# Paged sample attention in a hybrid decoder step: value products placed directly ahead of the scores two blocks on, value loads ahead of key loads

## What is computed

```python
k_past = cache_k[page_table].reshape(Bs, past_len, N_HEADS_B, HEAD_DIM_B)
v_past = cache_v[page_table].reshape(Bs, past_len, N_HEADS_B, HEAD_DIM_B)
...
z = jnp.einsum("bqhd,bkhd->bhqk", q_i.astype(f32), kf) * scale + bias
mask = (k_pos[None, :] < p_i[:, None])[None, None]
log_keep = jnp.where(mask, jax.nn.log_sigmoid(-z), 0.0)
log_rest = lax.cumsum(log_keep, axis=3, reverse=True) - log_keep
att = jnp.where(mask, jnp.exp(jax.nn.log_sigmoid(z) + log_rest), 0.0)
return jnp.einsum("bhqk,bkhd->bqhd", att, vf)
```

## Time and profile before

| what | value |
|---|---|
| median of 3 runs | 2033.95 us |
| lowest, highest | 2031.24, 2036.3 us |
| profiled execution: span from first to last instruction | 2041.4 us |
| mean granted TensorE clock, share of full speed | 0.978 |
| busy share of the span: PE, PEld, DVE, ACT, POOL | 93%, 80%, 50%, 40%, 12% |
| DMA: moved, mean rate | 505.53 MB, 248 GB/s |
| key loads of 1024 KB: issue to landing, median | 11.2 us |
| value loads of 1024 KB: issue to landing, median | 10.7 us |
| weight loads of 1024 KB: issue to landing, median | 6.1 us |

### The profile page before, as it was taken

How to read it: one execution, slowest core, us unless ns; L and a number is a source line. 1 busy time by engine, 2 the same in 40 slices (tenths; PEclk the granted TensorE clock), 3 DMA queues, 4 the chain that set the end, 5 groups by cost and what they waited for, 6 DMA issues and landing times.

```text
span 2041.4 us, 49327 instructions
## 1 busy us (share of the span) xinstructions
PE 1900.4 (93%) x20670; PEld 1626.6 (80%) x20670; DVE 1014.2 (50%) x1676; ACT 816.9 (40%) x1436; POOL 244.5 (12%) x308
## 2 busy tenths in 40 slices
PE   7999999999999999999999999999999899777797
PEld 6988999999888888879998777677777677334597
DVE  6644363544455555534454553343454344677344
ACT  4234232334455555623333333333333344655333
POOL 0200000000244434413200000000000000110032
PEclk9999999999999999989999999999999999998899
DMA  7435455544123222205488999999999999999641
GB/s 282 172 134 178 161 177 172 170 163 151 55 89 101 86 89 76 58 18 192 145 322 303 419 419 420 394 425 425 425 425 425 397 418 386 416 384 359 258 144 73
DMA packets 122382, 505.53 MB, mean 248 GB/s; under 512 B 15969, under 2 KB 55266, under 8 KB 76898
## 3 DMA queue, kind: packets, MB, share of 16 engines
q1 hardware_dynamic: 122178, 502.60, 64.4%
HBM read 470.24 MB, written 32.32 MB: 246 GB/s over the span
## 4 chain that ended last, share of the span: by engine, by line
PE 29%; DMA 18%; DVE 2%; issue 2%; SPq 1%; ACT 1%; DVEq 0%; ACTq 0%
DMA at_vraw<-in_cache_v 18%; PE psP L2499 7%; PE psP L2501 7%; PE psP L2500 7%; PE at_psO L2549 4%; PE at_psS L2528 3%; SPq L1912 1%; PE psP L2594 0%; PE at_psT L2540 0%; SPq L1930 0%; SPq L1952 0%; DVE at_o_new L2416 0%; ACT at_p_w L2219 0%; PE psP L2616 0%; ACT at_p_w L2217 0%
## 5 line engine op out<-in xcount | busy, mean ns | idle before, releaser
L2499 PE MATMUL psP<-xhi,whi 128*128 128x320 f32 x1488 | 476.3, 320 | 2.6 <-DVE xlo L2386 1.9
L2500 PE MATMUL psP<-xlo,whi 128*128 128x320 f32 x1488 | 461.0, 310 | 0.0
L2501 PE MATMUL psP<-xhi,wlo 128*128 128x320 f32 x1488 | 461.0, 310 | 0.0
L2499 PEld LDWEIGHTS psP<-xhi,whi 128*128 128x128 f32 x1488 | 280.8, 189 | 65.8 <-issue 65.1
L2261 DVE TENSOR_TENSOR wlo<-wraw,whi 128x2048 fp32r<-128x2048 f32 x92 | 213.0, 2315 | 206.8 <-ACT whi L2087 206.6
L2087 ACT ACTIVATE whi<-wraw 128x2048 fp32r<-128x2048 f32 x92 | 176.0, 1913 | 277.0 <-PE psP L2501 275.7
L2500 PEld LDWEIGHTS psP<-xlo,whi 128*128 128x128 f32 x1488 | 281.2, 189 | 0.1
L2501 PEld LDWEIGHTS psP<-xhi,wlo 128*128 128x128 f32 x1488 | 280.8, 189 | 0.0
L131 PE MATMUL psP<-xhi,whi 128*128 128x320 f32 x704 | 218.1, 310 | 3.0 <-DVE wlo L166 2.4
L132 PE MATMUL psP<-xlo,whi 128*128 128x320 f32 x704 | 217.5, 309 | 0.0
L133 PE MATMUL psP<-xhi,wlo 128*128 128x320 f32 x704 | 217.5, 309 | 0.0
(11 more groups left out here) (359 smaller groups left out, 3237.0 us busy)
## 6 DMA issues: line engine op xcount, KB each, us to landing
wraw<-in_weights SPq DMA_DIRECT2D x160, 1024.0 KB, 6.1
at_kraw<-in_cache_k SPq DMA_DIRECT2D x96, 1024.0 KB, 11.2
at_vraw<-in_cache_v SPq DMA_DIRECT2D x94, 1024.0 KB, 10.7
at_kraw<-in_cache_k SPq DMA_DIRECT2D x64, 512.0 KB, 9.7
at_vraw<-in_cache_v SPq DMA_DIRECT2D x62, 512.0 KB, 10.7
rw_s0t<-in_s0T SPq DMA_DIRECT2D x16, 256.0 KB, 4.0
o_wkv_s<-rw_SN SPq DMA_DIRECT2D x16, 256.0 KB, 2.2
resT<-in_xT SPq DMA_DIRECT2D x4, 640.0 KB, 5.9
```

The lines of the kernel that those rows point to most:

```text
L2499: pe.matmul(out, wh, c_.xhi[:, kc, :], start=(kc == 0), stop=False)
L2500: pe.matmul(out, wh, c_.xlo[:, kc, :], start=False, stop=False)
L2501: last = pe.matmul(out, wl, c_.xhi[:, kc, :], start=False, stop=(kc == NM - 1))
```

## The change

One function is new, and six places use it. The values of block `k`, and what hangs on them, are planned from `value_time` and not from `block_time(k, 1.5)`:

```diff
+def value_time(k, part=0.0):
+
+    return block_time(k, part + (1.995 if k < NK - 2 else 1.5))
+
+
 def sample_ended(b):
-    return block_time(NBLK * max(b, SHARING - 1) + NBLK - 1, 2.3)
+    return value_time(NBLK * max(b, SHARING - 1) + NBLK - 1, 0.8)
...
-                values = [(block_time(freed // KB, 1.6 + 0.2 * (freed % KB)), load_value, i // KB, i % KB)
+                values = [(value_time(freed // KB, 0.02 + 0.02 * (freed % KB)), load_value, i // KB, i % KB)
                           for i in range(VRING + 1, KB * (NK - 1)) for freed in (i - VRING - (i < EXTRA + 4),)]
...
             def finals():
                 for b in range(NB):
-                    yield block_time(NBLK * b + NBLK - 1, 1.9)
+                    yield value_time(NBLK * b + NBLK - 1, 0.4)
...
-                    yield block_time(NBLK * b + NBLK - 1, 2.25)
+                    yield value_time(NBLK * b + NBLK - 1, 0.75)
...
-                    yield block_time(k, 1.5)
+                    yield value_time(k)
                     pe.wait_ge(*((v_in[k % 2], loads_of(k)) if k < NK - 1 else (v_last, 16 * KB)))
...
                     if k % NBLK == NBLK - 1:
-                        yield block_time(k, 2.2)
+                        yield value_time(k, 0.7)
```

## The result

The change makes the kernel slower: 2063.72 us (median of 4 runs), against 2035.12 us for the kernel before on the same chip (4 runs), a ratio of 1.0125 with a 95% interval of 1.0099 to 1.0152. One of the four runs was a slow one, 4663.27 us; the other three took 2060.38, 2062.49 and 2064.94 us, and the ratio goes by these. The forecast was 2028.5 us with a range of 2020 to 2040 us, so it was wrong in its direction and its range. The profiled execution took 2064.94 us, its span is 2063.2 us, and its mean granted clock is 0.969 (0.978 before).

A forecast was written before the change was run, and what follows sets the result against it. Transfers were taken to bound the kernel from 1120 to 1905 us. Taking back 5.5 us of the DMA engines' dry time, with all other terms at 0, gave 2033.95 - 5.5 = 2028.5 us, range 2020 to 2040 us.

The forecast's parts named there:

- the bound of the stretch beside the heads: Beside the prompt's heads, transfers were taken as the bound, with DMA share 0.98 over 165 us.
- In steady flow this costs and gives nothing: Moving values directly ahead of scores on PE keeps the load order and was costed at 0 in steady flow.
- That stretch is full at 0.98, so this gives nothing by itself: Beside the heads, ending PE's 8.0 us of waits for ACT's copy saves no time, as transfers fill the stretch.
- rival D: PE's clock falls behind longer waits for value pages, slowing values to scores: up to +9 us, 2043 us; chance 0.17.
- rival A: The forecast itself: the DMA engines' dry time from 1120 to 1905 us shrinks, gaining 2 to 9.4 us; chance 0.52.
- No window with a share under 0.8: Sign of the forecast being right: no 5 us window from 1120 to 1905 us has a DMA share under 0.8.
- Fewer changes of matmul kind: On PE, 0.31 us saved for each of 62 blocks, 19 us, all spent waiting for values; costed at nothing.
- rival C: PE was the hidden bound, so the 19 us of matmul switches come off: 2015 us; chance 0.13.
- Turn and values apart: Among the heads, PE's 8.0 us of waits for ACT's copy of turned weights go; value pages are late next; gain 0.
- Value loads ahead of key loads: On SP, weight chunks and stores move ahead of the value loads; no transfer gets longer, cost nothing.
- Start and end: At the kernel's start 0, bounds -2 and +3 us; at its end 0, bound +2 us.
- A's fastest case: Lower end of the time range that the shrinking dry time alone gives, 2023.5 to 2032 us.

The follow-up runs named there:

- run 7: Kernel before, with only an eighth of every key and value page loaded from block 48 on: 2028.6 us (one run); scores 48 to 63 take 172.7 us.
- run 8: Changed kernel, with only an eighth of every key and value page loaded from block 48 on: 2053.86 us (one run); scores 48 to 63 take 206.5 us.
- run 1: Change kept for blocks 0 to 46 only, blocks 47 to 61 as in the kernel before: 2031.44 us, ratio 0.9963 to the kernel before.
- run 2: Change kept for blocks 47 to 61 only, blocks 0 to 46 as in the kernel before: 2067.42 us, ratio 1.0148 to the kernel before.
- run 3: Changed kernel's place of the values on PE, with all loads in the order of the kernel before: 2065.52 us, ratio 1.0118 to the kernel before.
- run 4: Values at their old place on PE, only the value loads where the change has them: 2047.27 us, ratio 1.0044 to the kernel before.
- run 6: Kernel before, with scores from block 49 on moved up directly behind the values at their old place: 2053.29 us, ratio 1.0057.
- run 5: Change kept for blocks 0 to 46; from block 47 values at 1.75 of a block, not 1.5 as before: 2045.09 us, ratio 1.0022 to the kernel before.
- run 9: Change kept for blocks 0 to 46; values of blocks 47 to 61 at 1.38, earlier than the old 1.5: 2040.7 us, ratio 1.0004 to the kernel before.

## Why the prediction was wrong

**The step that failed** is the bound of the stretch beside the heads, and with it two costs set at nothing: "In steady flow this costs and gives nothing" for the values' new place, and "That stretch is full at 0.98, so this gives nothing by itself" for the turn and the values. I took a full DMA share as proof that nothing else sets the pace. Run 7 shows that the transfers there hid a second bound only 8 us (4%) below them, so a loss on PE was covered for 8 us at most; of the 34 us between runs 7 and 8, 31 came through. For the projections I had named what stood behind the values and moved ahead of them; for the heads I had printed the ten rows and never asked who waits for them. These are links in chains that run PE, ACT, DVE, PE, and a lump of 3.7 to 5.8 us of values and scores holds all of them up at once, as the timeline above shows for one place. The other term that should have been in the sum is PE's clock beside the heads: it was costed only behind long waits for value pages (rival D), and by the estimate above it took 17.6 of the 31 us.

**The dry time (rival A)** was right only in part. Alone (run 1), the interleaved part gave a ratio of 0.9963, 7.5 us, against the 2.25 us that the forecast had for it. It didn't come as I described either. The windows of 5 us under a share of 0.9 from 1120 to 1740 us lost 4.5 us before, 2.9 in run 1 and 5.0 in the changed kernel, where new ones stand in place of the old:

```profile
1690.00:1695.00 5.00, 5.00 (x58) 2.88 (x53) 2.78 (x2) 0.41 (x1) 0.29 (x1) 1.00 0.65 221
1725.00:1730.00 5.00, 5.00 (x38) 1.77 (x41) 2.56 (x5) 1.98 (x5) 0.87 (x1) 0.70 0.51 148
```

That accounts for 1.6 us of run 1's gain. In the profiles 5.0 us of the gain lie between scores 0 and 48 and 3.8 us ahead of scores 0 (1081.0 us, not 1084.8), where the two kernels are the same, so that part is chance. Where the other 3.4 of the 5.0 us come from isn't shown; run 2, whose order there is the old one, also took 4.1 us less than the kernel before, so a single profile can't tell. In the changed kernel the key loads did leave soon behind the value loads, within 4.1 us at all but two of 60 places, so late keys were mended and the transfers ran dry elsewhere all the same. "No window with a share under 0.8" was wrong.

**Fewer changes of matmul kind.** Right beside the projections: values and scores are 1.74 us apart at 40 of 46 places there. Beside the heads they rarely are (1801.20 and 1802.95 is one of two such places), since the values run slow. PE's waits for value pages beside the projections grew, from 35.2 us to 43.2, just under the forecast's 45 to 50 (48.0 in run 1). PE was ahead and waited; rival C falls there. After:

```profile
PE at_psO L2554 <- DMA at_vraw<-in_cache_v: 43.2, 27, 3.8
```

**Turn and values apart.** The waits of 8.0 us for ACT's copy are gone, as forecast. Their place was taken not by value pages, as I wrote, but by 14.5 us for `at_p_attT` and 7.5 us for `at_z_new`.

**Value loads ahead of key loads.** Costed at nothing, and right for the change as it stands: with the values late, the old order of the loads (run 3) and the new one take 627.4 and 626.5 us beside the projections and 209.1 and 211.1 beside the heads, all within the scatter. Only with the values in their old place does it cost something (run 4).

**Start and end.** Nothing there: from scores 63 to the end it is 146.0 us before and 147.4 after. In the range, A's fastest case should have read 2024.6 us (2033.95 - 9.4) and not 2023.5; that changes nothing.

**Rival D** had the sign and one symptom, slow value groups becoming common (3 us or more in 11 of 64 blocks, 3 before), but neither place nor cause: it put them beside the projections, behind long waits for value pages, at +9 us. There the granted clock only fell from 0.99 to 0.97. Beside the heads there are no waits for value pages at all; the clock falls among many waits for ACT and DVE. That the Trainium skill, page "TensorE: Matmul & The Clock Gate", section "HAM oscillation — how this bites in real kernels", warns of groups that each wait for a transfer agrees with the symptom (842 ns for a value matmul in place of 630), though here the waits are for other engines, not transfers.

## What to carry to other kernels

A DMA share of 0.98 says that the transfers are a bound, not that they are the only one: cut the bytes to an eighth in a kernel of its own, and the next bound shows its distance, here 8 us of 180. Before moving a piece of work past others on an in-order engine, name for each stretch who is passed. In this kernel long independent matmuls (the projections) could be passed freely, short links of a chain between engines couldn't, and two pieces of 1.9 us put together cost more there than the same two pieces apart. A planned place that serves one stretch need not serve the next: the change confined to the projections (run 1) beats both kernels, at 0.9963 of the one before.

## What the runs showed of the hardware

The low clock cost more than I had thought for a stretch whose waits were mostly of 1 to 4 us, one over 5, none of them for a transfer. Beside the heads the mean granted clock went from 0.93 to 0.82 with PE's busy share nearly unchanged (77% before, 74% after): 13.4 us more not busy, 17.6 us more of busy time for the same instructions. In run 6 a single wait of PE in this stretch was longer than 3 us, and the mean clock was still 0.85. It was low in every kernel with late values or a lump there (0.83 in runs 2 and 3, 0.84 in 8, 0.85 in 6, 0.86 in 5), with full transfers and with hardly any, and 0.92 to 0.95 in the others (runs 1, 4, 7 and 9). Not explained is run 4: beside the projections its DMA share is 1.01 as everywhere, yet 410 GB/s pass and not 415.
